# Two projections behind a layer norm: four sets of 128 columns taken k by k, and VectorE's work of the norm in another order

## What is computed

```python
h = _layer_norm(jnp.concatenate([meta, x], axis=1), ln_in_g, ln_in_b)
for l in range(DEPTH):                                   # DEPTH = 2
    m = _mixer(h, cos, sin, topk, w_in[l], ...)          # begins with h @ w_in
    h = _layer_norm(ALPHA * h + m, ln1_g[l], ln1_b[l])
    f = _conv_ffn(h, w_up[l], conv_w[l], conv_b[l], w_down[l])   # begins with h @ w_up
    h = _layer_norm(ALPHA * h + f, ln2_g[l], ln2_b[l])
return h[:, N_META:, :]

def _layer_norm(x, g, b):
    mu = jnp.mean(xf, axis=-1, keepdims=True)
    var = jnp.mean(jnp.square(xf - mu), axis=-1, keepdims=True)
    y = (xf - mu) * lax.rsqrt(var + LN_EPS) * g + b
```

## Time and profile before

| | us |
|---|---|
| median of 3 runs | 2651.67 (2650.14 to 2654.08) |
| the profiled execution | 2649.61 |
| its span, first to last instruction | 2647.8 |
| PE busy | 2529.2 (96%) |
| DVE busy | 1784.7 (67%) |
| ACT busy | 1370.3 (52%) |
| TensorE clock granted, mean | 0.979 |
| norm 0, 1, 2, 3: DVE scales the first chunk at | 33.44, 543.30, 1356.71, 1860.79 |

### The profile page before, as it was taken

How to read it: one execution, slowest core, us unless ns; L and a number is a source line. 1 busy time by engine, 2 the same in 40 slices (tenths; PEclk the granted TensorE clock), 3 DMA queues, 4 the chain that set the end, 5 groups by cost and what they waited for, 6 DMA issues and landing times.

```text
span 2647.8 us, 54314 instructions
## 1 busy us (share of the span) xinstructions
PE 2529.2 (96%) x21018; PEld 2414.3 (91%) x21018; DVE 1784.7 (67%) x2820; ACT 1370.3 (52%) x2131; POOL 12.2 (0%) x21
## 2 busy tenths in 40 slices
PE   5999999989999999999989999998899999999997
PEld 4999788879999999999979997888899999998886
DVE  6887577776666666545578875877766666665555
ACT  5444465465556555433354444654666556653433
POOL 0000000000000000000000000000000000000000
PEclk8999999989999999999989999999999999999998
DMA  4433232435555555555534332333455555555553
GB/s 165 152 114 129 70 113 96 136 127 169 180 173 175 168 181 173 176 172 176 174 136 158 114 132 68 112 104 128 145 181 182 183 180 177 189 183 190 184 189 114
DMA packets 109723, 401.76 MB, mean 152 GB/s; under 512 B 12176, under 2 KB 12176, under 8 KB 109584
## 3 DMA queue, kind: packets, MB, share of 16 engines
q1 hardware_dynamic: 108432, 395.15, 45.6%
q0 software_dynamic: 1152, 4.63, 0.4%
HBM read 397.50 MB, written 2.23 MB: 151 GB/s over the span
## 4 chain that ended last, share of the span: by engine, by line
PE 86%; DVE 9%; ACT 3%; issue 2%; DMA 1%; SPq 0%; ACTq 0%; DVEq 0%
PE ps L440 19%; PE ps L441 18%; PE ps L442 18%; PE ps L456 6%; PE ps L559 4%; PE ps L561 4%; PE ps L560 4%; PE ps L458 3%; PE ps L711 3%; PE ps L524 1%; PE ps L698 1%; DVE h L1250 1%; DVE h L1231 1%; PE ps L677 1%; PE ps L533 1%
## 5 line engine op out<-in xcount | busy, mean ns | idle before, releaser
L821 ACT ACTIVATE w_hi<-raw 128x1024 fp32r<-128x1024 f32 x728 | 764.5, 1057 | 767.4 <-PE ps L442 521.4
L1154 DVE TENSOR_TENSOR w_lo<-raw,w_hi 128x1024 fp32r<-128x1024 f32 x528 | 638.4, 1223 | 507.3 <-ACT w_hi L821 507.1
L441 PE MATMUL ps<-x_lo,w_hi 128*128 128x272 f32 (+1 forms) x2944 | 841.8, 286 | 0.0
L442 PE MATMUL ps<-x_hi,w_hi 128*128 128x272 f32 (+1 forms) x2944 | 840.4, 285 | 0.0
L440 PE MATMUL ps<-x_hi,w_lo 128*128 128x272 f32 (+1 forms) x2816 | 807.1, 287 | 20.1 <-DVE x_lo L1255 19.7
L442 PEld LDWEIGHTS ps<-x_hi,w_hi 128*128 128x128 f32 x2944 | 556.3, 189 | 0.0
L441 PEld LDWEIGHTS ps<-x_lo,w_hi 128*128 128x128 f32 x2944 | 556.3, 189 | 0.0
L440 PEld LDWEIGHTS ps<-x_hi,w_lo 128*128 128x128 f32 x2816 | 531.9, 189 | 23.2 <-issue 16.9
L561 PE MATMUL ps<-x_hi,w_hi 128*128 128x272 f32 (+1 forms) x960 | 279.7, 291 | 0.0
L560 PE MATMUL ps<-x_lo,w_hi 128*128 128x272 f32 (+1 forms) x960 | 279.6, 291 | 0.0
L456 PE MATMUL ps<-g_both,w_hi 128*128 128x512 f32 x704 | 246.4, 394 | 0.0
(11 more groups left out here) (287 smaller groups left out, 3827.7 us busy)
## 6 DMA issues: line engine op xcount, KB each, us to landing
raw<-stream SPq DMA_DIRECT2D x744, 512.0 KB, 3.4
h<-x SPq DMA_DIRECT2D x4, 544.0 KB, 6.3
out<-h SPq DMA_DIRECT2D x4, 544.0 KB, 2.7
cst<-consts POOLq DMA_DIRECT2D x2, 724.0 KB, 6.4
wkv<-w_kv POOLq DMA_DIRECT2D x2, 512.0 KB, 7.8
b_st<-ssm_b POOLq DMA_DIRECT2D x2, 512.0 KB, 9.2
c_st<-ssm_c POOLq DMA_DIRECT2D x2, 512.0 KB, 10.6
par<-params SPq DMA_DIRECT2D x1, 562.0 KB, 12.1
```

The costliest lines, as they stand in the source:

```text
L441: pe.matmul(acc, w_hi[:, slot, kk, cols], lo, start=False, stop=False)
L442: mm = pe.matmul(acc, w_hi[:, slot, kk, cols], hi, start=False, stop=k == tiles - 1)
L821: act.activation(w_hi[:, slot, :, :], raw[:, slot, :, :], ACT.Copy).then_inc(hi_made, 1)
L1154: dve.tensor_tensor(w_low(phase, slot), raw[:, slot, :, :], w_hi[:, slot, :, :].bitcast(F32), ALU.subtract).then_inc(in_lo_made if phase = ...
```

## The change

Three things change; the arithmetic stays the same.

PE: the first two groups of "up" and the first four sets of "in" are now both taken by `first_blocks`: blocks are laid out so that the stream brings set-pair 0 k 0..3, set-pair 1 k 0..3, set-pair 0 k 4..7, set-pair 1 k 4..7, then k 8..11 and 12..15 of pair 0, then of pair 1 (`FIRST_BLOCKS`). The first four blocks are used two by two, so that each of the first four chunks of `x_lo` brings 24 matmuls. PE's wait for low parts stands ahead of each pair and asks for both. All four banks must be free at the start. The loop over "up" begins with its second body and has no wait for `x_lo` any more.

DVE: the norm's order is written out anew; the first shift removal is of one chunk and goes ahead of the reciprocal, the second of one, the others of two; low parts of the weights stand earlier.

ACT and DVE behind it: the reader of the first finished sets waits for the sixth block, not the fourth; tiles of the input projection's first four sets are read two at a time; the first pair of groups of the up-projection is taken out of the loop on both engines.

```diff
+WOVEN = 2 * WIDE
+FIRST_BLOCKS = [0, 4, 1, 5, 2, 3, 6, 7]
@@ products
-                    it = loop.enter_context(pe.Fori(0, groups // body)) if groups > body else 0
+                    it = loop.enter_context(pe.Fori(1, groups // body)) if groups > body else 0
@@ PE
+            def first_blocks(l, phase, places, lows, t0=0):
+                sets = [(FIRST_BLOCKS[n] // KB, (first_block(l, phase) + n) % SLOTS) for n in places]
+                b = FIRST_BLOCKS[places[0]] % KB
+                pe.wait_ge(lows, first_low(l, phase) + places[-1] + 1)
+                for kk in range(KB):
+                    k = b * KB + kk
+                    if k % 2 == 0:
+                        pe.wait_ge(xlo_made, CHUNKS * (2 * l + (phase == "up")) + k // 2 + 1)
+                    for p, slot in sets:
+                        lo_w = w_low(phase, slot).rearrange("p a b -> p (a b)").rearrange("p (k m) -> p k m", k=KB)
+                        for j in range(2):
...
+                        if kk == KB - 1:
+                            mm.then_inc(block_used, 1)
@@ in_blocks
+                    if n < WOVEN:
+                        if n == 0:
+                            pe.wait_ge(psum_free, first_group(l, "glu") + 2)
+                        if n in (0, 2):
+                            first_blocks(l, "in", (n, n + 1), in_lo_made)
+                        elif n >= 4:
+                            first_blocks(l, "in", (n,), in_lo_made)
+                        continue
@@ PE, behind layer_norm_sums(ln)
-                products(l, "up", x_parts, lambda k: (xlo_made, CHUNKS * ln + k // 2 + 1), LAST_T0[0] if l == DEPTH - 1 else 0)
+                pe.wait_ge(psum_free, first_group(l, "up") + 2)
+                for places in ((0, 1), (2, 3), (4,), (5,), (6,), (7,)):
+                    first_blocks(l, "up", places, lo_made, query_t0(l))
+                products(l, "up", x_parts, None, query_t0(l))
@@ ACT, read_tile
-                    act.wait_ge(block_used, first_block(l, "in") + n + 1)
+                    act.wait_ge(block_used, first_block(l, "in") + (n + 1 if n >= WOVEN else 6 if n < 6 else 8))
@@ ACT, convolve
-                    act.wait_ge(block_used, i * 4 + (first_block(l, "up") + 4 * (g + 1)))
+                    woven = 2 if isinstance(i, int) and i + g == 0 else 0
+                    act.wait_ge(block_used, i * 4 + (first_block(l, "up") + 4 * (g + 1) + woven))
@@ ACT (and the same on DVE with low_part)
-                with act.Fori(0, FT - 2, 2) as i:
+                for e in range(2):
+                    for n in range(4):
+                        cast(l, "up", 4 * (e + 1) + n)
+                    convolve(e, e)
+                with act.Fori(2, FT - 2, 2) as i:
@@ DVE, layer_norm (scale, low_x and low_w are the steps of before, unshift takes a number of chunks)
-                    unshifted = [unshift(0)]
+                first = unshift(0, 1) if n else None
                 dve.wait_ge(dev_made, n + 1)
                 mark(dve.reciprocal(rstd[:, :], rstd[:, :]))
                 after()
...
+                scale(0, first)
+                low_w(1)
+                if n:
+                    low_x(0)
+                    second = unshift(1, 1)
+                    scale(1, second)
+                    third = unshift(2, 2)
+                    scale(2, third)
+                    low_x(1)
+                    low_w(2)
...
+                else:
+                    scale(1)
+                    low_x(0)
+                    scale(2)
+                    low_x(1)
+                    low_w(2)
...
+                low_x(6)
+                low_x(7)
```

92 lines of the change are left out of this document (61 added, 31 removed).

## The result

The changed kernel takes **2656.39 us** (median of 15 runs, 2651.87 to 2657.92); the kernel before took 2650.41 in the same rounds (15 runs). The ratio is 1.0017, 95% interval 1.0010 to 1.0024: **4.5 us slower, between 2.7 and 6.4**. A second set of rounds gave 1.0016 (1.0006 to 1.0025). The profiled execution of the changed kernel happened to be its fastest one, 2651.87 us. So the two profiles shown differ by only 2.3 us, and I compare stretches of them, not their ends.

A forecast was written before the change was run, and what follows sets the result against it. DVE's queue was taken to set when the norm ends, and so block 4's start. Norm terms of +1.8 us and two clock falls of +4.0 gave +5.8, forecast 2657.5 us, range from below 2652.5 to 2660.5.

The forecast's parts named there:

- Norm 0: Input projection behind norm 0: low part 0 moves ahead of the reciprocal; -0.3 us, bounds 0 and -1.1.
- Norm 1, up to block 4: Reciprocal some 0.5 us earlier, ACT's end 0.8 later, table load of 1.28 gone: block 4 starts 0.5 us earlier.
- Norms 1 and 3, block 8: Up-projection: PE reaches block 8 before its low part; new waits of 0.4 us at norm 1, about 0.6 at norm 3.
- The clock: PE idles 3.8 us ahead of block 4, its clock falls: 2.0 us at each of norms 1 and 3, +4.0 together.
- Norm 2: More low parts ahead of the last scaling: ACT ends 1.9 us later, `abp` still ends last; +1.9, at least +0.4.
- Norm 3: Like norm 1 with 258 columns: 0.5 us earlier, about 0.6 of wait at block 8, clock fall 2.0 more.
- Norm 4: Same DVE work with one more shift removal, a drain and an instruction: +0.2 us.
- the first: Clock doesn't fall behind both waits ahead of block 4: 2655.5 us with one fall, 2653.5 with none; chance 0.25.
- The second: Block 4 ready when PE finishes blocks 0 to 3, waits become gain: about 2644 us, half of it 2649; chance 0.13.
- The third: Cold blocks behind norms 0 and 2 reach past `abp`: +2.0 us each, 2661.5; chance 0.12.

The follow-up runs named there:

- e1: Changed kernel with 20 extra matmuls keeping PE busy ahead of block 4 in each up-projection: 2655.30 us, ratio 1.0014 to the kernel before.
- e5: Changed kernel with the cast and low part of block 4 moved earlier at norms 1 and 3: 2649.47 us, ratio 0.9991 to the kernel before.
- e6: Changed kernel with block 4's cast and low part earlier at norms 1 and 3, norm 2's low parts 2 and 3 behind the last scaling: 2645.15 us.
- e7: Changed kernel with block 4's cast and low part earlier, mixer's projection as before except norm 2's half-wide first shift removal: 2645.32 us, ratio 0.9976.
- e2: Changed kernel with a tiny Silu on ACT ahead of block 4's cast at norms 1 and 3, restoring the table load: 2663.13 us, ratio 1.0045.
- f2: Changed kernel with the feed-forward part put back as before, leaving the mixer's part alone: 2656.34 us, ratio 1.0018 to the kernel before.

## Why the prediction came out

Forecast +5.8 us (2657.5); measured 2656.39, by the ratio +4.5 (2.7 to 6.4). The direction and the reason held; two terms were too large.

- **Norm 0**: forecast -0.3, measured -0.3 (139.92 against 140.22).
- **Norm 1, up to block 4**: first removal -0.5, measured -0.55; ACT's end of the norm 0.8 later, measured 0.55 (559.53 - 536.63 = 22.90 us from the variance to the first cast, where 562.22 - 539.87 = 22.35 led to the table load); the load gone. Behind its first matmul PE was cold for 5.8 us, not 4.6, and so waited only 0.56 us for low part 3, not 1.3. Block 4 was forecast 0.5 sooner and came 0.76 sooner (561.89 - 536.63 = 25.26 against 565.89 - 539.87 = 26.02). This was the argument's core: the order takes away waits in front of a block that isn't there yet. The waits between chunks, 20.1 us less the first ones in the earlier trace rows, did vanish, and 3.20 and 3.45 stood ahead of block 4 instead (forecast 3.8).
- **Norms 1 and 3, block 8**: forecast waits of 0.4 and 0.6, measured 0.2 (above) and 0.5 (0.59 us between the starts, of which 0.12 is the pace). The place and its releaser were right: low part 8 starts 574.49 - 570.89 = 3.60 us behind the taps, where I had taken 3.83 from the earlier trace rows. That is the difference.
- **The clock: the term that was mis-sized.** It did fall behind both waits. It was at 0.50 for 3.4 us and not for the 4.6 that the stretch behind norm 0 had shown, and a fall cost 1.5 us (e1), where I had 2.0; that is nearly the cheap end I had given (1.4). The way by which I decided that it would fall doesn't hold up: the changed kernel's second profile has 1.93 us of idle ahead of block 4 at norm 3, and a clock of 0.50 from 1.2 us behind its end:

```profile
1885.93 0.39 PE L477 MATMUL ps<-x_hi,w_lo 128*128 128x258 f32 x1 [1.93 <-DVE w_lo L1191]
```

```profile
1887.10:1890.50 3.40, 3.40 (x18) 3.40 (x17) 2.18 (x2) 0.46 (x2) 0.00 (x0) 0.50 0.79 272
```

  In the same norm of that profile the clock had fallen once before, two matmuls behind a wait of 2.06 us ahead of block 2, for 3.4 us:

```profile
1876.44 0.39 PE L477 MATMUL ps<-x_hi,w_lo 128*128 128x258 f32 x1 [2.06 <-DVE w_lo L1191]
```

  That fall cost nothing. It made PE's wait for block 4 shorter, 1.93 us where the first profile has 3.45; block 4 starts 24.26 us behind the reciprocal in both, and the stretches are 631.50 and 631.54. So a slower PE is paid for only where PE, and not VectorE's low part, is what ends last. The length of the one wait is no measure of whether the clock falls, as the earlier trace rows already said with one row against two. The Trainium skill (TensorE: Matmul & The Clock Gate, HAM oscillation) tells of a kernel whose waits of some 3 to 5 us each left TensorE cold for the burst behind. Here the clock was at 0.50 at once behind the wait of 3.45 us, behind that of 3.20 after three matmuls at the higher level, and behind this one of 1.93, shorter than those the page tells of, after eight.
- **Norm 2**: forecast +1.9 in all; measured 143.01 - 140.60 = +2.4 behind the reciprocal and -0.56 ahead of it, +1.85. `abp` did end last, with 1.04 us of wait for the earlier trace rows's 1.44, although PE had stood 6.76 us ahead of block 4.
- **Norm 3**: forecast +2.1 with its fall; measured +1.90 - 0.55 = +1.35. **Norm 4**: forecast +0.2; measured -0.56 + 0.8 = +0.2.

The sum of the measured terms is -0.3 + 1.1 + 1.85 + 1.35 + 0.2 = **+4.2**, and the ratios are 1.0017 and 1.0016. The forecast lies 1.6 above it: 1.0 for the two falls, 0.3 for block 8, 0.5 for block 4, less some 0.2 that came out larger. Between the medians of the first set stand 6.0 us, almost my 5.8. That agreement is better than the terms deserve.

**The rivals.** The clock didn't hold, so the first is out. The second, that the waits come back as gain, "decides from a low part 4 at 561.6", 20.7 us behind the reciprocal as it would come in the changed kernel. e5 put that part at 561.96 - 541.11 = 20.85, and a gain came: 8.2 us by stretches against the changed kernel, 6.8 by medians. The point was right, and the change misses it by 3.4 us of queue (560.61 + 1.22 - 537.62 = 24.21). Against the kernel before, e5 is only 4.0 us faster by stretches and 2.4 by the ratio, where the rival had 7.7; norm 2's loss is still in it, and e6 and e7, without most of that, come to 6.1 and 7.5 by stretches. The third, cold blocks that reach past `abp`, didn't occur: the clock was at 0.50 behind block 4 of norm 2 (first matmul 0.56), and `abp` was still later.

**What stays open.** The attention stretches, which no edit touches, take from 708.7 to 718.6 us in fourteen profiles. In the one stretch of 15 us shown above the clock is at 1.00 in one profile and at 0.89 in the other. Of the eight profiles with the k by k order behind norms 0 and 2, six have over 715.5; of the other six, one. e2 and f2 measure 3 to 4 us slower than their stretches say. Whether the later norm 2 shifts where the clock falls, or this is chance, these runs can't settle, with one profile for each kernel (two for the changed one) and 2.4 us of uncertainty on each ratio.

## What to carry to other kernels

When an order is changed to take waits out of a row of blocks, look first at when the block behind them can start, and move its preparation in the same edit: here one cast and one subtraction put a few operations ahead turned +4 us into -4. Of two consumers on one norm, the one with slack (here the mixer's projection, hidden in front of `abp`) shouldn't get work placed in front of the last scaling, on which the chain with no slack depends. And where a kernel's clock wanders by several microseconds outside of the edit, compare stretches between fixed instructions as well as medians: here equal ones repeated within 0.2 us, once 0.5, where the ratio was uncertain by 2.4.
